# End of the kernel and the norms between its halves in token-block order, a second gate diagonal, and the first down split beside the last up tile

## The reference

```python
u   = rmsnorm(x) * gain1 * (1 + scale_m) + shift_m        # shift, scale, gate: SiLU(cond) @ w_mod
mix = four head groups(u @ w_in)                          # attention A, RG-LRU, neighbourhood C, GQA D
x1  = x + rmsnorm(mix @ w_out) * gain2 * gate_m
v   = rmsnorm(x1) * gain3 * (1 + scale_f) + shift_f
h   = silu(v @ w_up[:, :5632]) * (v @ w_up[:, 5632:])
y   = x1 + rmsnorm(h @ w_down) * gain4 * gate_f
```

## Time and profile before

| | us |
|---|---|
| median of 3 executions (1846.70 to 1852.88) | 1848.35 |
| the profiled execution | 1848.33 |
| its span, first to last instruction | 1846.3 |
| TensorE busy | 1763.1 (95%) |
| VectorE busy | 946.2 (51%) |
| ScalarE busy | 655.6 (36%) |
| GpSimd busy | 126.2 (7%) |
| up matmuls after the last transposes, in the chain of waits | 730.19 for 720.74 |
| share of TensorE in the chain of waits | 92% |

### The profile page before, as it was taken

How to read it: one execution, slowest core, us unless ns; L and a number is a source line. 1 busy time by engine, 2 the same in 40 slices (tenths; PEclk the granted TensorE clock), 3 DMA queues, 4 the chain that set the end, 5 groups by cost and what they waited for, 6 DMA issues and landing times.

```text
span 1846.3 us, 21922 instructions
## 1 busy us (share of the span) xinstructions
PE 1763.1 (95%) x9163; PEld 1510.0 (82%) x9163; DVE 946.2 (51%) x1273; ACT 655.6 (36%) x930; POOL 126.2 (7%) x169
## 2 busy tenths in 40 slices
PE   4899999999999986999999999999999999999995
PEld 0666666677778866999999999999999888888884
DVE  5345468733556668356556633333333355555553
ACT  2322244443464334222222222222222345454541
POOL 1000024440300001000000000000000000000000
PEclk9999999999999998999999999999999999999998
DMA  9777866776322241444545443333333233333311
GB/s 376 284 281 306 329 254 263 284 275 261 130 104 95 92 160 62 166 167 177 204 183 205 171 150 122 129 130 122 137 115 137 97 132 127 125 133 118 137 69 69
DMA packets 46474, 317.31 MB, mean 172 GB/s; under 512 B 5420, under 2 KB 7864, under 8 KB 8936
## 3 DMA queue, kind: packets, MB, share of 16 engines
q1 hardware_dynamic: 43328, 298.99, 43.2%
q0 software_dynamic: 2720, 13.71, 2.1%
q10 hardware_dynamic: 328, 3.21, 0.5%
HBM read 310.50 MB, written 5.39 MB: 171 GB/s over the span
## 4 chain that ended last, share of the span: by engine, by line
PE 92%; DVE 4%; issue 1%; DMA 1%; ACT 1%; POOL 0%; DVEq 0%; SPq 0%; ACTq 0%
PE ps L1003 40%; PE ps L791 8%; PE ps L793 8%; PE ps L792 8%; PE ps L739 7%; PE ps L740 7%; PE ps L741 7%; PE ps L718 3%; PE ps L902 1%; PE ps L925 1%; DMA ident<-in_ident_c 1%; PE ps L959 1%; DVE wlo L1064 1%; PE ps L915 1%; PE ps L852 0%
## 5 line engine op out<-in xcount | busy, mean ns | idle before, releaser
L1064 DVE TENSOR_TENSOR wlo<-raw,whi 128x1024 fp32r<-128x1024 f32 x376 | 459.2, 1235 | 718.0 <-ACT whi L415 718.0
L415 ACT ACTIVATE whi<-raw 128x1024 fp32r<-128x1024 f32 x376 | 392.0, 1058 | 841.9 <-PE ps L1003 505.3
L1003 PE MATMUL ps<-h_hi,whi 128*128 128x384 f32 x1408 | 471.5, 335 | 0.0
L1003 PE MATMUL ps<-h_lo,whi 128*128 128x384 f32 x1408 | 470.3, 334 | 0.0
L1003 PE MATMUL ps<-h_hi,wlo 128*128 128x384 f32 x1408 | 470.3, 334 | 0.0
L791 PE MATMUL ps<-whi,h_hi 128*128 128x512 f32 x672 | 281.2, 418 | 9.8 <-DVE wlo L1064 9.8
L793 PE MATMUL ps<-wlo,h_hi 128*128 128x512 f32 x672 | 264.6, 394 | 0.0
L1003 PEld LDWEIGHTS ps<-h_lo,whi 128*128 128x128 f32 x1408 | 264.5, 188 | 0.0
L1003 PEld LDWEIGHTS ps<-h_hi,whi 128*128 128x128 f32 x1408 | 264.5, 188 | 0.0
L1003 PEld LDWEIGHTS ps<-h_hi,wlo 128*128 128x128 f32 x1408 | 264.4, 188 | 0.0
L792 PE MATMUL ps<-whi,h_lo 128*128 128x512 f32 x672 | 263.7, 392 | 0.0
(11 more groups left out here) (234 smaller groups left out, 1144.0 us busy)
## 6 DMA issues: line engine op xcount, KB each, us to landing
raw<-in_weights SPq DMA_DIRECT2D x284, 1024.0 KB, 4.9
xT<-in_x_t ACTq DMA_DIRECT2D x1, 3072.0 KB, 12.3
out<-x_sb POOLq DMA_DIRECT2D x3, 1024.0 KB, 4.7
x_sb<-in_x_sample POOLq DMA_DIRECT2D x1, 2048.0 KB, 11.0
sbc<-silu_rows POOLq DMA_DIRECT2D x1, 2048.0 KB, 8.0
gw<-in_lru_gate_w SPq DMA_DIRECT2D x4, 256.0 KB, 2.8
out<-U POOLq DMA_DIRECT2D x4, 256.0 KB, 5.7
nabias<-rpb_pad POOLq DMA_DIRECT2D x16, 64.0 KB, 3.5
```

What stands on the lines that cost most here:

```text
L415: nc.scalar.activation(whi[:, 2 * (g % RING) + b], raw[:, t % RAW, HK * b:HK * b + HK].rearrange("p k n -> p (k n)"), ACT.Copy).then_inc(w ...
L1003: return nc.tensor.matmul(ps[bank][:, 0:T], w[:, k % KH * P:(k % KH + 1) * P], xs[:, k, :], start=first, stop=last)
L1064: V.tensor_tensor(wlo[:, 2 * (t % RAW) + b], raw[:, t % RAW, HK * b:HK * b + HK].rearrange("p k n -> p (k n)"), whi[:, 2 * (g % RING) + b] ...
```

## The change

It rearranges four places. (1) `diag_b` is a second buffer for the diagonals of odd index in the out projection; the odd one is written at the start of the step, the even one at the end of the step before. (2) Between the halves, residual 0 stands ahead of the last block's add; x1 is squared in halves of 1024 columns; the norm scale is no longer multiplied into `xn` but stands in a diagonal for each block, placed between the residuals, and `x_transpose` uses three fp32 matmuls. (3) The first down tile's low splits stand before the last product of the up stage; `j_hi` of tile 0 waits for half of the last up tile only, and TensorE's wait for the last products moves to down tile 1. (4) The last down tile runs block by block, ScalarE squares its banks, VectorE multiplies banks by a gate that was copied to SBUF, each block has its own row scale, x is updated in halves, and SP's queue stores each half. Beside that, the factor 1/D moves into the squares, and two small operations of GpSimd (`lamt`, `neglam`) move to an earlier place.

```diff
-    dump = at("dump", [P, D], H0)
+    dump = at("dump", [P, 2 * TB, D // 2], H0)
+    ysd = at("ysd", [P, TB, NC], U0)
...
+                    part = slice(D // 2 * b, D // 2 * (b + 1))
+                    sp.wait_ge(fin, 2 * tb + b + 1)
+                    sp.dma_start(y_p[0, :, part] if tb == 0 else y_s[0, (tb - 1) * P:tb * P, part], x_sb[:, tb, part]).then_inc(out_st, 16)
+            sp.wait_ge(out_st, 2 * TB * 16)
 
 
...
             gap(STEPS - 1, 2)
             for tb in range(TB):
-                act.wait_ge(x1_ok, tb + 1)
-                if tb:
-                    act.wait_ge(sq_done, 4 + tb)
-                nc.scalar.activation(dump[:, :], x_sb[:, tb, :], ACT.Square, accum_out=xss[:, tb:tb + 1]).then_inc(sq_done, 1)
+                for b in range(2):
+                    act.wait_ge(x1_ok, 2 * tb + b + 1)
+                    nc.scalar.activation(dump[:, 2 * tb + b, :], x_sb[:, tb, D // 2 * b:D // 2 * (b + 1)], ACT.Square,
+                                         scale=D ** -0.5, accum_out=xsh[:, 2 * tb + b:2 * tb + b + 1]).then_inc(sq_done, 1)
...
                         act.wait_ge(h3_ok, KG * q + KG)
                     if v < 2:
-                        act.wait_ge(w_used, used("up", FK - 1, 1))
+                        act.wait_ge(w_used, used("up", FK - 1, 1) - 1 + v)
...
-            y_out(y2, 3, used("down", 3, KG2 - 1))
+            act.wait_ge(w_used, used("down", 3, 1))
+            act.wait_ge(g_ps, 16)
+            for j in range(2):
+                nc.scalar.activation(gate_sb[:, j, :], ps[7 - j][:, :], ACT.Copy).then_inc(gate_ok, 1)
+            for tb in range(TB):
+                act.wait_ge(o_ps, tb + 1)
+                nc.scalar.activation(ysd[:, tb, :], ps[3 + tb][:, :], ACT.Square, scale=D ** -0.5,
+                                     accum_out=yss[:, 4 * tb + 3:4 * tb + 4]).then_inc(y_sq, 1)
...
+            def last_tile(key, kg, bank, xh, xl, k_last):
+
+                parts = list(halves(TILE[key]))
+                for tb in range(TB):
+                    xs = slice(tb * P, (tb + 1) * P)
+                    acc = ps[bank + tb][:, :]
+                    for b, wh, wl in parts:
+                        for kk in range(HK):
+                            k = KG * kg + HK * b + kk
+                            cols = slice(kk * NC, (kk + 1) * NC)
+                            nc.tensor.matmul(acc, xh[:, kk + HK * b, xs], wh[:, cols], start=False, stop=False)
+                            nc.tensor.matmul(acc, xl[:, kk + HK * b, xs], wh[:, cols], start=False, stop=False)
+                            ins = nc.tensor.matmul(acc, xh[:, kk + HK * b, xs], wl[:, cols], start=False, stop=(k == k_last))
+                    ins.then_inc(o_ps, 1)
 
...
                 b = ps[xt_bank(k)]
-                for tb in range(TB - 1):
-                    nc.tensor.transpose(b[:, tb * P:(tb + 1) * P], xn[:, tb, k * P:(k + 1) * P], ident[:, :])
-                nc.tensor.matmul(b[:, 2 * P:T], x_sb[:, 2, k * P:(k + 1) * P], diag[:, 0, :], start=True, stop=True,
-                                 skip_group_check=True).then_inc(xt_ps, 1)
+                for tb in range(TB):
+                    ins = nc.tensor.matmul(b[:, tb * P:(tb + 1) * P], x_sb[:, tb, k * P:(k + 1) * P], diag[:, tb, :],
+                                           start=True, stop=True, skip_group_check=True)
+                ins.then_inc(xt_ps, 1)
...
-                nc.tensor.matmul(ps[gain_bank(idx)][:, :], ones[:, :], diag[:, :, :].rearrange("p f n -> p (f n)"),
+                src = diag_b if idx < 8 and idx % 2 else diag
+                nc.tensor.matmul(ps[gain_bank(idx)][:, :], ones[:, :], src[:, :, :].rearrange("p f n -> p (f n)"),
...
                     v = n * KG2 + q
                     pe.wait_ge(jl, v + 1)
-                    if v == 0:
-                        pe.wait_ge(h3_ok, FK)
+                    if v < 2:
+                        pe.wait_ge(h3_ok, FK - 2 + 2 * v)
+                    if v == 4 * KG2 - 1:
+                        last_tile(("down", n, q), q, 3 * (n % 2), j_hi[v % 2], j_lo[v % 2], FK - 1)
+                        break
...
             def diagonal(g0, n, cond, idx):
 
-                if idx:
+                if idx >= 8:
                     dve.wait_ge(g_ps, idx)
+                elif idx >= 2:
+                    dve.wait_ge(g_ps, idx - 1)
+                dst = diag_b if idx < 8 and idx % 2 else diag
                 for f in range(4):
-                    ins = V.tensor_scalar(diag[:, f, :], ident[:, :], modc[:, g0 + 4 * n + f, cond:cond + 1], None, ALU.mult)
+                    ins = V.tensor_scalar(dst[:, f, :], ident[:, :], modc[:, g0 + 4 * n + f, cond:cond + 1], None, ALU.mult)
...
                     gap(s - 1, 2)
                 if n >= 0:
-                    diagonal(G_M, n, 1, 2 * n)
+                    diagonal(G_M, n, 0, 2 * n + 1)
...
                 if s >= EARLY * KG:
                     gap(s, 0)
-                    if n >= 0:
-                        diagonal(G_M, n, 0, 2 * n + 1)
...
-
-            gap(STEPS - 1, 2)
+                if -1 <= n < OUT_N - 1:
+                    diagonal(G_M, n + 1, 1, 2 * n + 2)
+
             dve.wait_ge(x1_in, 32)
-            for tb in range(TB):
+
+            def residual(tb):
+
                 y1_gate(3, tb)
                 dve.wait_ge(y_g, 9 + tb + 1)
                 dve.wait_ge(rs_done, 2 + tb)
                 for n in range(4):
                     x = x_sb[:, tb, n * NC:n * NC + NC]
                     ins = V.scalar_tensor_tensor(x, y1[n][:, tb, :], yrs[:, tb:tb + 1], x, ALU.mult, ALU.add)
-                ins.then_inc(x1_ok, 1)
-            for tb in range(TB - 1):
-                dve.wait_ge(x1_ok, tb + 1)
+                    if n % 2:
+                        ins.then_inc(x1_ok, 1)
+
+            def norm_diagonal(tb):
+
                 dve.wait_ge(rs_done, 5 + tb)
-                V.tensor_scalar(xn[:, tb, :], x_sb[:, tb, :], xrs[:, tb:tb + 1], None, ALU.mult).then_inc(xn_done, 1)
-            dve.wait_ge(rs_done, 7)
-            V.tensor_scalar(diag[:, 0, :], ident[:, :], xrs[:, 2:3], None, ALU.mult).then_inc(xn_done, 1)
+                if tb == 0:
+                    dve.wait_ge(g_ps, 8)
+                V.tensor_scalar(diag[:, tb, :], ident[:, :], xrs[:, tb:tb + 1], None, ALU.mult).then_inc(xn_done, 1)
+
+            residual(0)
+            gap(STEPS - 1, 2)
+            residual(1)
+            norm_diagonal(0)
+            residual(2)
+            norm_diagonal(1)
+            norm_diagonal(2)
             lo("up", 0, 1)
...
+            def j_low(v):
+
+                q = v % KG2
+                dve.wait_ge(jh, v + 1)
+                V.tensor_tensor(j_lo[v % 2][:, :, :], h3T[:, KG * q:KG * q + KG, :], j_hi[v % 2][:, :, :].bitcast(F32),
+                                ALU.subtract).then_inc(jl, 1)
...
                 if f + 1 < FK:
                     lo("up", f + 1, 1)
+                if f == FK - 1:
+                    lo("down", 0, 0)
+                    j_low(0)
...
+                    if v:
+                        lo("down", n, q)
+                        j_low(v)
...
-            y_gate(y2, 3, 14)
-            dve.wait_ge(y_g, 24)
-            dve.wait_ge(rs_done, 8)
+            dve.wait_ge(gate_ok, 2)
+            dve.wait_ge(y_g, 21)
             for tb in range(TB):
-                V.scalar_tensor_tensor(x_sb[:, tb, :], y2[:, tb, :], yrs[:, tb:tb + 1], x_sb[:, tb, :],
-                                       ALU.mult, ALU.add).then_inc(fin, 1)
+                dve.wait_ge(y_sq, 12 + tb + 1)
+                V.tensor_tensor(y2[:, tb, 3 * NC:], ps[3 + tb][:, :], gate_sb[:, 0 if tb == 0 else 1, :], ALU.mult).then_inc(y_g, 1)
+                dve.wait_ge(y_g, 21 + tb + 1)
+                dve.wait_ge(rs_done, 8 + tb)
+                for b in range(2):
+                    c = slice(D // 2 * b, D // 2 * (b + 1))
+                    V.scalar_tensor_tensor(x_sb[:, tb, c], y2[:, tb, c], yrs[:, tb:tb + 1], x_sb[:, tb, c],
+                                           ALU.mult, ALU.add).then_inc(fin, 1)
...
+                    pool.wait_ge(lam_e, 1)
+                    link(G.tensor_tensor(lamt[:, 0:1], lamt[:, 3:4], lamt[:, 2:3], ALU.subtract))
+                    G.tensor_scalar(neglam[:, :], lamt[:, 0:1], 1.0, -LAM_INIT, ALU.mult, ALU.add).then_inc(lam_ok, 1)
...
+            def row_means(count, done):
+
                 ys = yss[:, :].rearrange("p (t n) -> p t n", n=4)
-                halves(ys, 2)
+                pool.wait_ge(count, done)
                 link(G.tensor_tensor(yrs[:, :], ys[:, :, 0], ys[:, :, 1], ALU.add))
-                inv_rms(yrs[:, :], yrs[:, :], 3, D).then_inc(rs_done, 1)
...
+            def row_scale(tb):
+
+                r = yrs[:, tb:tb + 1]
+                link(G.tensor_tensor(r, r, yss[:, 4 * tb + 3:4 * tb + 4], ALU.add))
+                G.tensor_tensor(r, r, negh[:, 0:1], ALU.pow).then_inc(rs_done, 1)
+
+            row_means(y_sq, 9)
```

(37 more changed lines are left out.)

22 lines of the change are left out of this document (6 added, 16 removed).

## The result

The changed kernel takes 1824.27 us (median of 4, 1822.48 to 1824.36) against 1848.59 for the kernel before, measured with it: a ratio of 0.9863 with a 95% interval of 0.9845 to 0.9881. The sign was right. By stages, the middle gave 3.55 us for 4.0 and the first down tile 7.56 for 7.6; the end was wrong by 4.6 us.

What follows compares the result with a forecast made beforehand. TensorE, busy 95% of the span, bounds the kernel, so only its idle time and the stretch behind its last matmul can be had: 4.0 + 7.6 + 8.2 = 19.8 us off 1848.35 gives 1828.5 us, range 1824.5 to 1835.

Steps and rivals of the forecast that it cites:

- the middle: Out projection to up loop: second diagonal and token-block order gain 7.4 us, transposes as matmuls cost 3.4; net 4.0 us.
- parts 1 and 4: Second diagonal ends three out-projection stalls, 5.9 us; early first down split removes gap and slow matmuls, 7.6 us.
- The three places: TensorE's waits: 14.6 us before the transposes, 5.1 us in three for a diagonal, 4.6 us at the first down tile.
- Part 2: Between the halves, token-block order: transposes begin at about 701.65 instead of 709.07, only 1.5 us of it from the order.
- Part 3: Transposes as fp32 matmuls: first five blocks cost 1.3 us, eleven in the up loop 2.4, less 0.25; 3.4 us cost.
- Rival D: Clock rises as the transposes begin, thirty records take 3.2 us, and the store lands in 2.8 us: 1825.5 us; chance 0.07.
- Part 5: Behind the last matmul: last update 6.95 us earlier, last store 1.3 us; sum 8.2 us, ends 6.5 and 9.
- A: Rival: transposes and the new wait eat the gain between the halves, 0.5 us instead of 4: 1832 us; chance 0.13.
- B: Rival: DVE's halves, GpSimd's scales or small stores bind the end, which gives 5 us: 1831.7 us; chance 0.12.
- C: Rival: first down tile still waits and the clock falls as before, 4.9 us of 7.6 lost: 1833.4 us; chance 0.04.
- E: Rival: without rests the granted clock falls in the down phase; four tiles lose 28.8 us: 1857.3 us; chance 0.02.
- F: Rival: another wait replaces the three diagonals and the tail, gain under 5.5 us; chance 0.04.

Runs made afterwards that it cites:

- the fastest version: Changed kernel with the norm scale multiplied into xn and transposes as before, all three scales behind residual 2, no warm matmuls: 1818.97 us.

## Why the prediction was right or wrong

**What bounds the kernel, parts 1 and 4: right.** The three places were the ones that moved. The stalls gave 5.90 us for 5.9, the first down tile 7.56 for 7.6, with the 2.86 us of slow matmuls behind the gap as a true part of it: undoing the early split costs 7.4 us in the trace, and the slow matmuls are there again.

**Part 2, the order: right in mechanism, 0.3 us low.** The late add (1.76 us for 1.75), the new wait on the diagonal of block 0 (0.71 for 1.1) and the start of the transposes (701.34 for 701.65) are all in the trace. GpSimd's add and power took 0.44 and 0.55 us there, one below the bounds of 0.55 to 0.93 and one at their low end; VectorE stood still during the power. Taking the wait away gives 1.0 us.

**Part 3, the matmuls for transposes: right, 0.7 us too cheap.** It cost 4.2 us (1.77 and 2.41) for 3.4. The step that was off is the clock's rise: 6.04 us for the first five against 5.55, near the bound of 6.4 for all low. With part 2 too low by 0.3 the middle came out only 0.4 off, and that is in part luck. Executions of the same code scatter from 4.8 to 6.0, so the half microsecond was not to be forecast from one row. The turn of the up loop is 1.73 us where 1.70 was said. Rival D's first half, an early rise, didn't happen in the change: the granted clock was 0.50 for 5.7 us from the restart. Whether plain matmuls bring the rise forward, as the prediction worked out from the Trainium skill's "TensorE: Matmul & The Clock Gate" (Part 4: PE-mode transpose), these runs leave open: behind a cold restart it came after 3.0 to 5.7 us in nine traces with thirty plain records, and after 4.8 to 5.0 us in four with pairs of transposes and matmuls.

**Part 5, the end: wrong by 4.6 us, in two steps.** VectorE's side was right to 0.05 us, 7.00 for 6.95. The first failed step is "in between lies 3.5 for 512 KB", a load's time put on a store: from issue to landing it took 2.7 us, outside the bounds of 2.8 to 4.9 given for it. From last update to last byte 2.40 us were gained instead of 1.3. Two runs account for most of it: 0.86 us for SP's queue instead of GpSimd's at 1 MB (4.66 to 3.80), and 1.1 us for half the size (3.37 to 2.26). The 0.43 between them lie between two kernels that both store 1 MB from SP's queue, the blocks 2.2 us apart in one and 3.1 to 3.3 in the other; no run shows the cause. The estimate by the Trainium skill's "DMA: Bandwidth & Descriptors" (Anatomy of one DMA), 3.2 us, stood between mine and the measured 2.7; the page gives its numbers for DMAs from GpSimd's queue, and this store came from SP's.

The second is the larger: "I leave the 4.3 us". I took what stands behind the last store for a fixed cost of ending a program, because nothing in the trace of before could be put against it. The text named the right doubt, that these 4.3 us were GpSimd's own, as something that would make the forecast wrong, and gave it neither a price nor a rival nor room in the range. The runs show that 3.4 us of it hang on GpSimd being last: 1.2 us stand behind the last byte in the change, and 3.2 us come back both when GpSimd only waits for SP's stores and when it fills memory instead. Why GpSimd takes so long stays open.

**The chances.** A (middle at 0.5) and B (end at 5) looked to the slow side for unknowns, and the range ended at 1824.5 below, since what could be gained behind the last store had been costed at nothing. Of A's conditions one held, the up loop was slowed by 0.24 us a turn instead of 0.215, but it cost 0.3 us and not 3.5. D's second half held, the store landed in 2.7 us, and D's time of 1825.5 came nearest to the measured one, though only its smaller half, the store, had a part in that. C, E and F left no trace.

## What to carry to other kernels

Ask which engine ends last, not only which store lands last: here a kernel whose last wait is GpSimd's ends 3 us later than one whose last wait is SP's. A cost that is idle on every engine and follows the last work is not thereby fixed; if a change moves the last work to another engine, it needs a bound down to zero. Price both sides of an exchange: here the diagonals cost 4.1 us in matmuls to save 1.0 us of waiting for VectorE. And an engine warmed or made faster ahead of a wait gives nothing unless what feeds it is also early: the fastest version left the low clock alone and balanced TensorE's slow transposes against VectorE's first split.

## What the runs showed of the hardware

- From GpSimd's last work to the end of the span it took 3.76 us behind a fill. Where GpSimd waits for the last store, whichever queue made it, 4.4 to 4.6 us stand behind the last byte; with SP last, 1.0 to 1.2 us.
- A store of 512 KB from SP's queue landed 2.7 us after its issue (median of six), one of 1 MB after 3.9 to 4.1 us (median of three, in two kernels).
- TensorE idle for 1.88 us, which followed an idle 0.61 us after 2.4 us of work, was followed by a granted clock of 0.50 for 3.4 us, while behind three stalls of 1.71 us, 12 us apart, it stayed at 1.00.
- GpSimd's power on one column took 0.54 to 0.58 us with VectorE idle or reading PSUM, and 0.93 to 1.76 us beside VectorE's updates and multiplications from SBUF (0.93, 1.76 in the same trace at 704.77, 1.43 in the change's tail, above).
